# Gate and up of a feed-forward chunk by seven block products in place of eight

## The reference

```python
D_MODEL = 1024; SEQ = 512; CTX_LEN = 256; D_FF = 2752
def swiglu(h, wg, wu, wd):
    return (jax.nn.silu(h @ wg) * (h @ wu)) @ wd

def ffn_sub(h, m, sub, j, p):
    y = swiglu(sandwich_in(h, m, sub, p), p['w_gate'][j], p['w_up'][j], p['w_down'][j])
    return sandwich_out(h, y, m, sub, p, 0.5)
```

## Time and profile before

| | us |
|---|---|
| median of three runs | 3056.74 (3053.74 to 3060.01) |
| span of the profiled execution | 3053.8 |
| TensorE busy, share | 2912.8, 95% |
| VectorE busy, share | 1639.7, 54% |
| ScalarE busy, share | 1017.2, 33% |
| POOL busy, share | 329.7, 11% |
| mean granted TensorE clock | 0.979 of full |

### The profile page before, as it was taken

How to read it: one execution, slowest core, us unless ns; L and a number is a source line. 1 busy time by engine, 2 the same in 40 slices (tenths; PEclk the granted TensorE clock), 3 DMA queues, 4 the chain that set the end, 5 groups by cost and what they waited for, 6 DMA issues and landing times. The chain is left out here.

```text
span 3053.8 us, 48883 instructions
## 1 busy us (share of the span) xinstructions
PE 2912.8 (95%) x17780; PEld 2769.2 (91%) x17780; DVE 1639.7 (54%) x2869; ACT 1017.2 (33%) x1714; POOL 329.7 (11%) x323
## 2 busy tenths in 40 slices
PE   6999999999998899999999999999999998899997
PEld 6999999979876889999999899999988876899997
DVE  4576565666346563465336676545566446643334
ACT  4212112444436352221224312212353545532233
POOL 2000000320003150000005000000150002500002
PEclk8999999999999999999999999999999999999999
DMA  6444444332200232344324344424432200433333
GB/s 230 126 130 124 117 126 136 111 87 63 70 8 32 61 95 59 97 124 116 83 63 121 106 125 125 123 73 134 117 107 63 85 14 26 131 96 98 93 94 111
DMA packets 457428, 297.61 MB, mean 97 GB/s; under 512 B 35342, under 2 KB 412532, under 8 KB 457276
## 3 DMA queue, kind: packets, MB, share of 16 engines
q1 hardware_dynamic: 454352, 288.92, 32.7%
q10 hardware_dynamic: 2924, 6.70, 0.6%
HBM read 293.23 MB, written 2.32 MB: 97 GB/s over the span
## 5 line engine op out<-in xcount | busy, mean ns | idle before, releaser
L1889 PE MATMUL ps<-hn,wsp 128*128 128x384 f32 (+1 forms) x3136 | 1029.7, 328 | 33.5 <-DVE hn L1422 20.2
L1890 PE MATMUL ps<-hn,wsp 128*128 128x384 f32 (+1 forms) x3136 | 1020.9, 326 | 0.0
L1891 PE MATMUL ps<-hn,wsp 128*128 128x384 f32 (+1 forms) x3136 | 1020.5, 325 | 0.0
L1334 DVE TENSOR_TENSOR wsp<-raw,wsp 128x1024 fp32r<-128x1024 f32 x364 | 451.5, 1240 | 459.8 <-ACT wsp L892 459.7
L1889 PEld LDWEIGHTS ps<-hn,wsp 128*128 128x128 f32 x3136 | 596.7, 190 | 47.8 <-issue 21.6
L1890 PEld LDWEIGHTS ps<-hn,wsp 128*128 128x128 f32 x3136 | 597.5, 191 | 0.0
L1891 PEld LDWEIGHTS ps<-hn,wsp 128*128 128x128 f32 x3136 | 597.1, 190 | 0.0
L892 ACT ACTIVATE wsp<-raw 128x1024 fp32r<-128x1024 f32 x404 | 425.1, 1052 | 486.3 <-PE ps L1891 458.1
L1889 PE MATMUL ps<-aT,wsp 128*128 128x384 f32 (+1 forms) x1344 | 439.3, 327 | 15.2 <-DVE wsp L1334 11.2
L1890 PE MATMUL ps<-aT,wsp 128*128 128x384 f32 (+1 forms) x1344 | 434.9, 324 | 0.0
L1891 PE MATMUL ps<-aT,wsp 128*128 128x384 f32 (+1 forms) x1344 | 434.6, 323 | 0.0
(11 more groups left out here) (231 smaller groups left out, 2968.9 us busy)
## 6 DMA issues: line engine op xcount, KB each, us to landing
modw<-in_w_mod SPq DMA_DIRECT2D x144, 512.0 KB, 4.2
raw<-in_ffn_w_gate SPq DMA_DIRECT2D x188, 256.0 KB, 3.5
raw<-in_ffn_w_up SPq DMA_DIRECT2D x188, 256.0 KB, 4.1
raw<-in_ffn_w_down SPq DMA_DIRECT2D x64, 448.0 KB, 3.4
raw<-in_w_in SPq DMA_DIRECT2D x96, 256.0 KB, 3.0
raw<-in_ffn_w_down SPq DMA_DIRECT2D x64, 256.0 KB, 4.1
raw<-in_w_out SPq DMA_DIRECT2D x64, 256.0 KB, 3.1
raw<-in_ffn_w_down SPq DMA_DIRECT2D x64, 192.0 KB, 3.6
```

What stands on the lines that cost most here:

```text
L1334: dve.tensor_tensor(wsp[:, cs, 1, 0:width], raw[:, slot, 0:width], wsp[:, cs, 0, 0:width].bitcast(F32), ALU.subtract).then_inc(wlo_done, 1)
L1889: pe.matmul(dst, w(0), x(0), start=first, stop=False)
L1890: pe.matmul(dst, w(0), x(1), start=False, stop=False)
L1891: return pe.matmul(dst, w(1), x(0), start=False, stop=last)
```

## The change

A chunk's gate and up are seen as a product of 2 x 2 blocks: gate and up against the lower and the upper 512 input features, and these against the two halves of the tokens. It is made with seven block products of 4 slices x 3 matmuls (84 matmuls) and sums, after Strassen and Winograd. Three products take weight blocks as they are, four take sums (`wsum`, and one written over the up tile in `raw`); three of the inputs are sums of `hn` blocks as well. This holds for the chunks of groups 1 to 3 in feed-forwards (0, 1), (1, 0) and (1, 1), and of group 3 in (0, 0) (`classical_groups`): 7 + 17 + 17 + 17 = 58 chunks.

- POOL makes 40 sums of `hn` slices per feed-forward (`sums_of_inputs`), when the second half of the norm is done, and per chunk four 512-wide sums of weights (`sums_of_weights`).
- The split input sums need room: `tD` lies over `xT`, so the residual is stored to HBM at the start of a feed-forward and loaded again before its post norm (`spill`, `x_back`); `tF` lies over `yF`, `tS` over `wsum`, and the difference of the late blocks replaces its first half in `hn`.
- ScalarE and VectorE split each of the seven weight operands of a chunk (512 wide) into a slot of `wsp`, four slots in turn (`operand_slot`, where some slots are skipped so that the tiles after a group find their place).
- VectorE combines the products with seven additions, ScalarE copies the first product. PSUM banks 0 to 3 serve seven products.
- The groups are 5, 5, 5 and 7 chunks; the half chunk is now in group 0. There is one more down pass per feed-forward; the matmuls in all down passes are as many as before.
- Modulation quarters are placed per step (`MOD_AT`), in all as many as before. The loops over chunks and down steps are unrolled.

```diff
--- before.py
+++ after.py
-GROUPS = [(0, 6), (6, 8), (14, 8)]
-GMAX = 8
+GROUPS = [(0, 5), (4, 5), (9, 5), (14, 7)]
+UP_TILES = [5, 10, 10, 14]
+SLOTS, OWN_SLOTS = 7, 5
+QUARTERS = 7
+def classical_groups(l, j): return 3 if (l, j) == (0, 0) else 1
...
+def operand_slot(G, m):
+    return (m + min(m // QUARTERS, 1 if G == 5 else 3)) % 4
...
+MOD_AT = {
+    (0, 0): {(0, UP): [2, 2, 0], (0, DOWN): [1] * KD, (1, UP): [2, 2, 4, 2, 2], (1, DOWN): [1] * KD,
+             (2, UP): [2, 2, 4, 2, 2], (2, DOWN): [1] * KD, (3, UP): [1, 1, 1, 1, 0, 0, 0]},
+    (0, 1): {(0, DOWN): [1] * KD, (1, UP): [1, 1, 1, 1, 0], (1, DOWN): [1] * KD, (2, UP): [1, 1, 1, 1, 0],
+             (2, DOWN): [1] * KD, (3, UP): [1, 1, 1, 1, 0, 0, 0]},
+}
+MOD_AT[1, 0] = MOD_AT[0, 1]
...
+        spill = nc.dram_tensor("spill", (P, KD, T), F32).ap()
+        tD = overlay("tD", [P, 2, 2, KD // 2, HW], F32R)
         xT = sb("xT", [P, KD, T])
...
-            aT = sb("aT", [P, 2, GMAX, T], F32R, s)
+            tA = sb("tA", [P, 2, KD // 2, HW], F32R, s)
+            tS = overlay("tS", [P, KD // 2, HW])
+            wsum = sb("wsum", [P, 3, KD // 2 * P], F32, s)
+            aT = overlay("aT", [P, SLOTS, 2, T], F32R)
+            sb("aT_stays", [P, OWN_SLOTS, 2, T], F32R, s)
+            tF = overlay("tF", [P, 3, KD // 2, HW])
             yF = sb("yF", [P, KD, T], F32, s)
...
+                pool.wait_ge(hlo_done, KD * (pre_event(l, 2 * j, 1) + 1))
+                f1, f2, f4 = tF[:, 0], tF[:, 1], tF[:, 2]
+                for k in range(h):
+                    put(k, f1, late(0, k), low(0, k), ALU.subtract, 0)
+                for k in range(h):
+                    put(k, tS, late(1, k), low(1, k), ALU.subtract, 0)
+                for k in range(h):
+                    put(k, f1, f1[:, k, 0:w], tS[:, k, 0:w], ALU.add, 2)
...
+                    put(k, f4, f4[:, k, 0:w], low(1, h + k), ALU.add, 9)
...
+                for i in range(G):
+                    tg, tu = t0 + 2 * i, t0 + 2 * i + 1
+                    gate, up = raw[:, tg % RAW], raw[:, tu % RAW]
+                    if i == 0:
+                        pool.wait_ge(tlo_done, 4 * (2 * l + j + 1))
+                        pool.wait_ge(wlo_done, splits_before(t0 - 2) + RAW)
+                    pool.wait_ge(raw_in[tg % RAW], 32 * (tg // RAW + 1))
+                    pool.wait_ge(raw_in[tu % RAW], 32 * (tu // RAW + 1))
+                    if i > 0:
+                        pool.wait_ge(wlo_done, e0 + QUARTERS * (i - 1) + 4 + RAW)
+                    pool.tensor_tensor(wsum[:, 0], up[:, 0:W], up[:, W:2 * W], ALU.add).then_inc(wsum_done, 1)
+                    pool.wait_ge(wsum_done, s0 + 4 * i + 1)
+                    pool.tensor_tensor(wsum[:, 1], wsum[:, 0], gate[:, 0:W], ALU.subtract).then_inc(wsum_done, 1)
+                    pool.tensor_tensor(up[:, 0:W], gate[:, 0:W], up[:, 0:W], ALU.subtract).then_inc(wsum_done, 1)
+                    pool.wait_ge(wsum_done, s0 + 4 * i + 2)
+                    if i > 0:
+                        pool.wait_ge(wlo_done, e0 + QUARTERS * (i - 1) + 7 + RAW)
+                    pool.tensor_tensor(wsum[:, 2], gate[:, W:2 * W], wsum[:, 1], ALU.subtract).then_inc(wsum_done, 1)
...
+                act.dma_start(spill[:, :, hv[0][0]:T], xT[:, :, hv[0][0]:T]).then_inc(x_spilled, 16)
...
+                    act.wait_ge(unit_done, u0 + 1)
+                    if c > 0:
+                        act.wait_ge(comb_done, 7 * c - 2)
+                    act.activation(p1[:, 0:w], ps[:, 0, 0:w], ACT.Copy).then_inc(part_out, 1)
+                    ahead(m0 + 4)
+                    ahead(m0 + 5)
+                    ahead(m0 + 6)
+                    ahead(m0 + 7)
+                    act.wait_ge(comb_done, 7 * c + 5)
+                    act.activation(sg2[0][:, 0:w], sg2[0][:, 0:w], ACT.Silu).then_inc(silu_done, 1)
+                    ahead(m0 + 8)
+                    ahead(m0 + 9)
+                    if g == len(GROUPS) - 1 and i == OWN_SLOTS:
+                        act.wait_ge(mod_sum, mods_after(l, j))
+                    act.wait_ge(amul_done, q + 3)
+                    act.activation(aT[:, i, 0, a0:a0 + w], af2[0][:, 0:w], ACT.Copy).then_inc(ahi_done, 1)
+                    act.wait_ge(comb_done, 7 * c + 7)
+                    act.activation(sg2[1][:, 0:w], sg2[1][:, 0:w], ACT.Silu).then_inc(silu_done, 1)
+                    ahead(m0 + 10)
+                    act.wait_ge(amul_done, q + 4)
+                    act.activation(aT[:, i, 0, a1:a1 + w], af2[1][:, 0:w], ACT.Copy).then_inc(ahi_done, 1)
...
+                    if g == last:
+                        act.wait_ge(unit_done, units_before(last_tile0(l, 2 * j)))
+                        for n, (a, w) in enumerate(hv):
+                            act.dma_start(xT[:, :, a:a + w], spill[:, :, a:a + w]).then_inc(x_back[n], 16)
...
+                    if sub != 1:
+                        dve.wait_ge(x_back[n], 16 * (2 * l + sub // 2 + 1))
...
+                    low(m0 + 4)
+                    dve.wait_ge(part_out, c + 1)
+                    dve.wait_ge(unit_done, u0 + 2)
+                    dve.tensor_tensor(p16[:, 0:w], ps[:, 1, 0:w], p1[:, 0:w], ALU.add).then_inc(comb_done, 1)
+                    low(m0 + 5)
+                    dve.wait_ge(unit_done, u0 + 3)
+                    dve.wait_ge(comb_done, 7 * c + 1)
+                    dve.tensor_tensor(p167[:, 0:w], ps[:, 2, 0:w], p16[:, 0:w], ALU.add).then_inc(comb_done, 1)
+                    low(m0 + 6)
+                    dve.wait_ge(unit_done, u0 + 4)
+                    dve.tensor_tensor(p16[:, 0:w], ps[:, 3, 0:w], p16[:, 0:w], ALU.add).then_inc(comb_done, 1)
+                    dve.wait_ge(comb_done, 7 * c + 2)
+                    dve.wait_ge(ahi_done, q)
+                    dve.tensor_tensor(af2[1][:, 0:w], ps[:, 3, 0:w], p167[:, 0:w], ALU.add).then_inc(comb_done, 1)
+                    low(m0 + 7)
+                    dve.wait_ge(unit_done, u0 + 5)
+                    dve.wait_ge(amul_done, q + 2)
+                    dve.tensor_tensor(sg2[0][:, 0:w], ps[:, 0, 0:w], p1[:, 0:w], ALU.add).then_inc(comb_done, 1)
+                    reduce_last()
+                    mods(g, UP, i)
+                    low(m0 + 8)
+                    dve.wait_ge(unit_done, u0 + 6)
+                    dve.tensor_tensor(af2[0][:, 0:w], ps[:, 2, 0:w], p167[:, 0:w], ALU.add).then_inc(comb_done, 1)
+                    low(m0 + 9)
+                    dve.wait_ge(silu_done, q + 3)
+                    dve.wait_ge(comb_done, 7 * c + 6)
+                    dve.tensor_tensor(af2[0][:, 0:w], af2[0][:, 0:w], sg2[0][:, 0:w], ALU.mult).then_inc(amul_done, 1)
+                    dve.wait_ge(unit_done, u0 + 7)
+                    dve.tensor_tensor(sg2[1][:, 0:w], ps[:, 3, 0:w], p16[:, 0:w], ALU.add).then_inc(comb_done, 1)
+                    low(m0 + 10)
+                    dve.wait_ge(ahi_done, q + 1)
+                    dve.tensor_tensor(aT[:, i, 1, a0:a0 + w], af2[0][:, 0:w], aT[:, i, 0, a0:a0 + w].bitcast(F32),
+                                      ALU.subtract).then_inc(alo_done, 1)
+                    dve.wait_ge(silu_done, q + 4)
+                    dve.tensor_tensor(af2[1][:, 0:w], af2[1][:, 0:w], sg2[1][:, 0:w], ALU.mult).then_inc(amul_done, 1)
+                    dve.wait_ge(ahi_done, q + 2)
+                    dve.tensor_tensor(aT[:, i, 1, a1:a1 + w], af2[1][:, 0:w], aT[:, i, 0, a1:a1 + w].bitcast(F32),
+                                      ALU.subtract).then_inc(alo_done, 1)
...
+                            input_lo(tD[:, 0, 1, :, 0:w], tD[:, 0, 0, :, 0:w], tF[:, 1], w, 2)
+                            input_lo(tD[:, 1, 1, :, 0:w], tD[:, 1, 0, :, 0:w], tF[:, 2], w, 3)
...
+                def product(t0, G, m, bank, x):
+                    z = operand_slot(G, m)
+                    pe.wait_ge(wlo_done, splits_before(t0) + m + 1 + RAW)
+                    K = KD // 2
+                    for k in range(K):
+                        ins = three(ps[:, bank, 0:hv[0][1]], weight((t0 + z // 2) % 2, (z % 2 * K + k) * P),
+                                    lambda p: x(p, k), k == 0, k == K - 1)
+                    ins.then_inc(unit_done, 1)
+                def seven(t0, G, i, g):
+                    q = pairs_before(l, j, g) + 2 * i
+                    c = seven_before(l, j, g) + i
+                    m0, K = QUARTERS * i, KD // 2
+                    (a0, w), (a1, _) = hv
+                    if i == 0:
+                        pe.wait_ge(amul_done, q + 2)
+                        pe.wait_ge(tlo_done, 4 * (2 * l + j + 1))
+                    else:
+                        pe.wait_ge(comb_done, 7 * c - 2)
+                    product(t0, G, m0, 0, lambda p, k: hn[:, p, k, a0:a0 + w])
+                    product(t0, G, m0 + 1, 1, lambda p, k: tD[:, 0, p, k, 0:w])
+                    if i > 0:
+                        pe.wait_ge(comb_done, 7 * c - 1)
+                    product(t0, G, m0 + 2, 2, lambda p, k: hn[:, p, k, a1:a1 + w])
```

(72 more changed lines are left out.)

532 lines of the change are left out of this document (313 added, 219 removed).

## The result

The changed kernel takes 3178.35 us (median of 4, 3176.19 to 3183.94), the kernel before, run beside it, 3056.99 (3053.74 to 3060.01): ratio 1.0405, 95% interval 1.0385 to 1.0425. It is slower by 121 us where 50 were forecast, and outside the range.

A forecast was written before the change was run, and what follows sets the result against it. TensorE, 95% busy, bounds the kernel before; after the change VectorE's rounds with ScalarE and POOL set the pace. Terms sum to +50 us on 3053.8, with 2.9 around the span 3107 us, range 3005 to 3155.

The forecast's parts named there:

- Removed matmuls, -109: TensorE, 58 chunks: 12 fewer matmuls each at 0.1724 us (wide) or 0.1176 us (narrow), 109 us in all.
- The ring without POOL: VectorE-ScalarE round trips per chunk with POOL free: 14.9 us wide with a modulation quarter, 11.5 us at 256 wide.
- The sums, +1.9 wide and +2.4 narrow: POOL's four weight sums per chunk exclude VectorE's SBUF-only splits, adding 1.9 us a wide round, 2.4 a narrow one.
- the last rival: POOL takes every second turn against VectorE, or TensorE slows: +52 us more, 3160 us, chance 0.14.
- "POOL doesn't disturb", 3013: Rival: POOL's sums fall into VectorE's idle time, so the kernel gains 44 us, 3013 us; chance 0.26.
- Group edges, +7 - 2: First and last chunks of groups: skipped slot and wait for the last activation, +7 us wide, -2 at 256.
- The down steps of groups of 5: no stall, though the spare time is gone: Down phases of groups of 5: VectorE's 4.5 us fit into TensorE's 5.2 us per step, so no stall.
- The last pass and tail, +5: Last passes lose 5.5 us of matmuls to earlier down phases; half does not come back in the tail, +5 us.
- POOL's sums of inputs, hidden: Group 0: POOL's 40 additions take 41 to 47 us, hidden within TensorE's 54 us until the down products.
- The +12 for VectorE's splits of them: Group 0's down phase: VectorE's 1536-wide splits of input sums delay the first evacuation, 3 us per feed-forward, +12 us.
- The residual, 0: Residual stored to HBM and loaded back four times: hidden, zero cost, up to 4 x 8 us if uncovered.
- The narrow feed-forward, +42 with its edges: Layer 1's second feed-forward, 17 chunks at 256: rounds of 13.9 us, +44 us, with edges of -2.

The follow-up runs named there:

- e3: Changed kernel with eight products in all chunks and no sums, keeping the new groups, quarter plan and residual in HBM: 3080.52 us, 1.0071 of the kernel before.
- e2: Changed kernel with POOL's four weight sums per chunk cut to 4 columns, raw blocks split instead, all waits kept: 3051.12 us, 0.9983 of the kernel before.
- e1: Changed kernel with SyncE issuing the next seven-product group's first gate and up tiles before the down phase's last two modulation loads: 3141.05 us, 1.0270 of the kernel before.
- e5: Changed kernel with ScalarE's splits of operands 8 and 10 before the silus, VectorE's split of operand 10 behind the first low part: 3083.18 us, 1.0085.
- e6: Changed kernel with POOL's 40 input sums per feed-forward cut to 4 columns, columns of hn used instead: 3168.69 us, 1.0367 of the kernel before.
- e4: Changed kernel with eight products in layer 1's second feed-forward alone, its input sums left out: 3140.36 us, 1.0271 of the kernel before.

## Why the prediction missed

The runs split the 121 us. Before to e3, +24. From e3 to e2, -29: chunks at e2's rounds in place of e3's give 41 x (16.64 - 14.31) + 17 x (11.36 - 11.10) = -100. Against it stand four edges: the first rounds of groups, 19.4 and 13.5 us where 14.31 and a unit's transposes of 0.95, and 11.10, would do, 7 x 4.1 + 3 x 2.4 = 36; late tiles 14 (the wait before the transposes is 29.8 us, 16.0 in e3); the wait for a group's last activation 11.0, in ten waits (none in e3); and the first copies of down phases 9 (10.4 against 1.8). Together -30. From e2 to the changed kernel, +127: 104 in the rounds and 22 more of the late tiles (51.8 against 29.8). The late tiles come to 36 us by these waits; e1 gave 37.

- **Removed matmuls, -109: right in kind.** e2's wide rounds are at TensorE's pace, 14.3 us; the narrow ones, at 11.1, are not at its 9.9, as forecast. The pace of 0.1724 us comes from a count in a stretch; by starts it is 0.1734, which changes no term by more than 1 us.
- **The ring without POOL: wide too long.** 14.9 us forecast, at most 14.31 measured. From the last combining addition (1281.67) the gate's addition comes 9.06 us later in e2 where the walk had 9.4, since the hand-overs are each a little shorter, and a quarter without a reduction takes 2.65, not 2.86. Narrow: 11.5 forecast, 11.10 measured.
- **The sums, +1.9 wide and +2.4 narrow: the exclusion right, its placement failed.** I had VectorE keep its turn while it has work. It doesn't, as e5's rows show: the instruction that loses its turn was the multiply, on the chain, and not only splits. A steady wide round has 2.6 of it and a narrow one 2.9, nearer to the 2.8 to 3.0 that the prediction gave if POOL gets every second turn, the last rival's mechanism. In the wide round this error and the one above cancel, which is why 16.8 met 16.93: luck. Over the 34 wide intervals the mean is 1.9 all the same, since the first and last rounds of a group lose less (1.1 and at most 1.6 us); so this step is not what was missing from the time.
- **"POOL doesn't disturb", 3013:** the run that makes it true gave 3051; that rival too had the edges wrong.
- **Group edges, +7 - 2: failed, mis-sized.** I counted 0.65 us for the first round's skipped slot. The round is 3.6 us longer than a steady one with POOL (20.5 against 16.93) and 5.1 without (19.4 against 14.31). e2's rows say from what: the slot alone is 1.8, and the waits for TensorE's products and the unit's reduction come on top. The waits for a group's last activation are 11.0 us in ten, also in e2. No run changed either of the two by itself.
- **"The down steps of groups of 5: no stall, though the spare time is gone": failed.** e3's 24 us hold 14 more of the wait before the transposes (16.0 against 2.3). 4.5 us of VectorE's work in 5.2 fits on average, but the last quarter has only the last unit to hide behind. The last pass and tail, +5: right. They got 17.6 us shorter with 22 us of matmuls moved away.
- **SyncE's queue: missing, the largest step that failed.** The prediction has no term for it. I read "in order" for VectorE and not for SyncE. The group's first tiles stand behind two loads that wait for VectorE; before, a tile's DMA led straight to ScalarE's and VectorE's split; the change put POOL's sums between, which put operand 1's split 3.2 us behind operand 0's, in front of a VectorE that holds the quarter TensorE waits for. It is 37 us by e1, half of the 71 by which the median missed. By my estimate the first rounds (7 x 2.95 + 3 x 1.4 = 25) and the 11 us of that wait which e1 leaves are about the rest.
- **POOL's sums of inputs, hidden: nearly.** 10 us by e6 over four feed-forwards. The +12 for VectorE's splits of them had no run of its own, but the trace bears it out (the changed kernel, at the start of a down phase; its four waits are 2.8, 2.8, 2.8 and 2.2 us):

```profile
1210.88 3.43 DVE L1768 TENSOR_TENSOR tD<-tF,tD 128x1536 fp32r<-128x1536 f32 x2
1214.34 0.56 DVE L1677 COPY yF<-ps 128x384 f32<-128x384 f32 x1
...
PE ps L2179 <- DVE yF L1677: 10.6, 4, 2.8
```

- **The +2 for the chunk with four quarters and the -7 for hidden transposes** had no run of their own.
- **The residual, 0: not refuted** (2 to 6.5 us, unsettled). **The narrow feed-forward, +42 with its edges: right in sum,** 38 by e4.

The Trainium skill (SBUF — State Buffer, "Who interferes with whom") says that a VectorE instruction with two SBUF inputs contends with a POOL instruction that reads SBUF, that the shared pair is an exclusive lock, and that whoever issues first holds it for the whole instruction, the other being fully blocked. The trace agrees: POOL's sum from 1419.72 ends at 1421.17, and the multiply queued at 1419.93 ends at 1421.58: with its own 0.55 us it started at 1421.03, some 0.14 before POOL's end, the same 0.15 that the two rows of the tail had given.

## What to carry to other kernels

Before work is given to an idle engine, write down which instruction releases it and what stands next and next but one behind that instruction on the other engine that shares its port; swapping two instructions there, with ScalarE's split moved ahead to match, was worth 79 us of 3178. When a step is put between a DMA and its first user, follow the DMA back through its queue, past everything that its issuing engine waits for. And walk through the first round of a pipelined group by itself, with its waits for the first products, and multiply by the number of groups: a steady round says nothing of it.
